# Second norm's scale applied after the feed-forward products in a two-model transformer kernel, with buffers and weight splits moved to suit

## Chip, cores and metric

The kernel runs on one core of a Trainium2 chip. Its metric is the device time of one execution in microseconds (us), the median of three runs. TensorE is PE in the rows, VectorE DVE, ScalarE ACT, GpSimd POOL, SyncE SP.

## What is computed

Two transformer layers, then a second model's block (gated delta rule and dilated attention). Only the layers are touched. Per layer, on x of 512 tokens by 1024:

```python
def rms_norm(x, g):
    xf = x.astype(jnp.float32)
    y = xf * lax.rsqrt(jnp.mean(xf * xf, axis=-1, keepdims=True) + EPS)
    return (y * g.astype(jnp.float32)).astype(x.dtype)

for l in range(DEPTH):                       # DEPTH = 2
    h = rms_norm(x, norm1[l]); proj = h @ w_in[l]
    ...                                      # four attention groups a, b, c, d
    mixed = jnp.concatenate([o_a, o_b, o_c, o_d], axis=-1)
    x = x + mixed @ w_out[l]
    h2 = rms_norm(x, norm2[l])
    x = x + jnp.square(jax.nn.relu(h2 @ w_up[l])) @ w_down[l]
```

## The kernel before

Nearly all work is matmuls of 128 by 128 by 512. For fp32 accuracy each operand is a pair: a high part rounded to fp32r and the rest (low). `product` (L180) issues three matmuls for one product: high by high (L182), high by low (L183), low by high (L184).

**Weights** stream in items of 512 KB through `WeightRing` (L99). SP sends an item into one of four raw slots once the item four earlier is split (L141). ACT rounds it into one of three pair slots (`high`, L152), for which the item three earlier must be used up by PE. DVE subtracts for the low part (`low`, L161). `high(act, i)` and `low(dve, i)` bring the split up to item i + 2. All engines work their queues in order, and the order is written out by hand: a wait holds everything behind it on its engine.

**Front**: the projections of the first norm; PE, ACT and DVE weave 26 weight steps with other work by a table. Its last step is finished inside attention, at p = `HOLD` = 1 (`held`).

**Attention** (L665): 64 jobs in 32 pairs. In round p, PE issues the scores of pair p (L701, L704), the values product of pair p - 4 (L737) and the transposes of pair p - 3 (L718). Scores of pair p need the exps of pair p - 2 done, since there are four score banks. DVE takes the maximum (L768), negates and scales it (L774), inverts the sum (L801); ACT exponentiates (L856) and copies (L865); POOL normalises (L895). Every eight jobs one chunk of `mixed` is stored, high by ACT (L870), low by DVE (L806), into `operand`. `fill` lets PE compute one chunk of the output product (12 matmuls) at p = 34 and at p = 35, after the transposes; it needs all exps done (the banks 0 to 3) and that chunk stored.

**Output product and second norm** (`OutputProducts`, `Residual`): columns 0 to 511 are products over chunks 0 to 7 into banks 0 to 3. Then columns 512 to 1023 into banks 4 to 7: one weight item for all four token tiles, then the last three items tile by tile (18 matmuls each). After each tile DVE adds to x (L603), ACT squares and sums (L452), DVE adds the halves (L457), ACT takes the root (L462), DVE inverts (L468) and scales the whole row (L477), PE transposes it (L505, 8 at a time, behind the next tile's matmuls), ACT and DVE store high (L514) and low (L526) in `operand`. The last tile's transposes have no matmuls left to hide behind; PE issues 24 and 36 dummy matmuls around them (`keep_busy`, L96) and then waits for all of `operand`.

**Feed-forward** (`mlp`): two halves of the 4096 hidden features, each an up projection (`UpProjection`, relu and square) and a down product added to x (L1315; the last half in `finish_dve`, L603), followed by the next norm with the same code. In layer 1 that tail norms twice (L472, L492).

Of the kernel before, what the change touches and what calls it, by code (L numbers as in the profile page):

```python
# [25 lines left out]
F32 = mybir.dt.float32  # L26
# [378 lines left out]
class Norm:  # L405
# [5 lines left out]
    def __init__(self, psum, x, weights, ident, eps, small, work, operand, sems, again=None, ident_half=None):  # L411
# [7 lines left out]
        self.again = again  # L419
# [115 lines left out]
class Residual(Norm):  # L535
# [49 lines left out]
    def add(self, dve, c, t, end, gate=None):  # L585
# [17 lines left out]
        dve.tensor_tensor(self.x[:, t, cols], prod, self.x[:, t, cols], ALU.add).then_inc(self.summed, 1)  # L603
# [61 lines left out]
def attention(block, psum, jobs, stores, ident, ident_half, probs, probs_t, stats, sems, besides=None, ready={},  # L665
# [24 lines left out]
    def _(pe):  # L690
# [51 lines left out]
        for p in range(pairs + STORE + 1):  # L742
# [16 lines left out]
            if fill is not None and p in (pairs + TURN - 1, pairs + VALUES - 1):  # L759
                fill(pe)  # L760

    @block.vector
    def _(dve):
# [59 lines left out]
        for p in range(pairs + STORE + 1):  # L823
# [21 lines left out]
    def _(act):  # L845
# [26 lines left out]
        for p in range(pairs + STORE + 1):  # L872
# [48 lines left out]
def product_by_channels(pe, psum, banks, weights, pair, chunks, written=None):  # L921
# [3 lines left out]
    for i in range(2):  # L925
        w = weights.take(pe)
        n = w[0].shape[1]
        for h, bank in enumerate(banks):
            for kk in range(n):
                if written is not None and h == 0:  # L930
# [3 lines left out]
                             stop=(k + kk == chunks - 1))  # L934
        k += n
# [19 lines left out]

class OutputProducts:
# [5 lines left out]
    def __init__(self, part, prefix, psum, x, weights, ident, ident_half, eps, small, work, lhs, per_half):  # L962
        self.per_half, self.weights, self.lhs, self.psum = per_half, weights, lhs, psum
        self.block = part.block
        self.tail = Residual(psum, x, weights, ident, eps, small, work, lhs, part.sems(prefix, TAIL_SEMS),
                             ident_half=ident_half)
        self.first = self.start = None

    def first_half(self, pe, stored_low, banks_freed):

        k, self.start = 0, self.weights.taken
        for i in range(self.per_half):
            w = self.weights.take(pe)
            for kk in range(w[0].shape[1]):
# [3 lines left out]
                for t in range(T):  # L978
                    tile = slice(t * P, (t + 1) * P)
                    mm = product(pe, self.psum[:, t, 0:w[0].shape[2]], [self.lhs[:, k, j, tile] for j in (0, 1)],  # L980
                                 [w[j][:, kk, :] for j in (0, 1)], start=(k == 0), stop=(k == KD - 1))
# [3 lines left out]
                yield  # L985

# [7 lines left out]

    def rest(self, rows_read, gain_row):
        start, per_half, weights, tail = self.start, self.per_half, self.weights, self.tail

        @self.block.sync
        def _(sp):
            weights.send(sp, start + 1)  # L1000
            sp.wait_ge(*rows_read)
            tail.load_gain(sp, gain_row)
            weights.send(sp, start + 2 * per_half - 1)
            tail.gain_loaded(sp)
# [2299 lines left out]
```

## Time and profile before

| | |
|---|---|
| median of 3 runs | 2093.86 us (2090.22 to 2101.56) |
| profiled execution | 2088.93 us |
| its span | 2087.2 us |
| mean granted TensorE clock | 0.987 |
| PE busy | 2009.6 us, 96% |
| DVE, ACT, POOL busy | 53%, 40%, 17% |
| DMA queue of the weights | 196.53 MB, 30.7% of 16 engines' span |

The span is the profiled execution without what lies around it (1.7 us). PE's busy time counts each matmul from its start to a modelled end, and these overlap; so 96% says that PE seldom stands still, not how much of its time is needed.

### The profile page before, as it was taken

To read this page: it belongs to the slowest core of one execution; us is meant where nothing else is said; L and a number is where in the kernel's file an instruction comes from. 1 tells how busy PE (TensorE), PEld (TensorE's weight loads), DVE (VectorE), ACT (ScalarE), POOL (GpSimd) and SP (SyncE) were. 2 spreads that over 40 slices of the span, in tenths; PEclk is the share of its full clock that TensorE was granted. 3 is DMA by queue.
4 is the path that set the end of the run, shared out by engine and by line. 5 is a ranking of instruction groups with operands and counts; after the bars stand their busy time and mean duration, and the time that the engine had idled before them with its cause. 6 is when DMAs were issued, how large, how long until landed. Compare 5 with 4: busy or idle time off the path is not lost. (4 is left out here: it accounts for less than half of the span.)

```text
span 2087.2 us, 27674 instructions
## 1 busy us (share of the span) xinstructions
PE 2009.6 (96%) x10604; PEld 1618.6 (78%) x10608; DVE 1115.6 (53%) x2039; ACT 836.0 (40%) x1744; POOL 360.1 (17%) x345
## 2 busy tenths in 40 slices
PE   8999999999999999999999999899999999999997
PEld 7776588888887877567888888688787887886776
DVE  5788634423434489835542543579765331425555
ACT  4455634312323344653321332454433334534632
POOL 1336700000000153750000000003030320004300
PEclk9999999999999999999999999999999999999999
DMA  6321022323232432012543433232225323341232
GB/s 190 98 75 52 1 71 92 110 93 91 91 120 71 121 100 80 11 41 81 192 162 93 170 118 111 75 101 83 79 77 146 79 66 99 92 140 41 81 121 81
DMA packets 177524, 198.29 MB, mean 95 GB/s; under 512 B 38755, under 2 KB 140786, under 8 KB 176882
## 3 DMA queue, kind: packets, MB, share of 16 engines
q1 hardware_dynamic: 177394, 196.53, 30.7%
q8 instruction: 85, 1.39, 0.3%
q14 instruction: 45, 0.37, 0.1%
HBM read 180.74 MB, written 11.55 MB: 92 GB/s over the span
## 5 line engine op out<-in xcount | busy, mean ns | idle before, releaser
L161 DVE TENSOR_TENSOR weight_pairs<-weight_ring,weight_pairs 128x1024 fp32r<-128x1024 f32 (+4 forms) x293 | 355.7, 1216 | 411.6 <-ACT weight_pairs L152 411.1
L182 PE MATMUL psum<-operand,weight_pairs 128*128 128x512 f32 x1320 | 526.8, 399 | 12.4 <-PEq L230 8.8
L152 ACT ACTIVATE weight_pairs<-weight_ring 128x1024 fp32r<-128x1024 f32 (+4 forms) x293 | 303.4, 1038 | 538.5 <-PE psum L184 523.6
L184 PE MATMUL psum<-operand,weight_pairs 128*128 128x512 f32 x1320 | 517.2, 392 | 0.0
L183 PE MATMUL psum<-operand,weight_pairs 128*128 128x512 f32 x1320 | 517.1, 392 | 0.0
L182 PEld LDWEIGHTS psum<-operand,weight_pairs 128*128 128x128 f32 x1320 | 249.3, 189 | 72.8 <-issue 19.4
L184 PEld LDWEIGHTS psum<-operand,weight_pairs 128*128 128x128 f32 x1320 | 248.6, 188 | 53.6
L183 PEld LDWEIGHTS psum<-operand,weight_pairs 128*128 128x128 f32 x1320 | 249.2, 189 | 50.9 <-issue 1.0
L895 POOL TENSOR_SCALAR probs<-probs,stats 128x128 f32<-128x128 f32 (+3 forms) x176 | 160.9, 930 | 239.4 <-DVE stats L801 239.1
L182 PE MATMUL psum<-weight_pairs,hidden 128*128 128x512 f32 x512 | 200.8, 392 | 0.0
L184 PE MATMUL psum<-weight_pairs,hidden 128*128 128x512 f32 x512 | 199.9, 391 | 0.0
L183 PE MATMUL psum<-weight_pairs,hidden 128*128 128x512 f32 x512 | 199.7, 390 | 0.0
L182 PE MATMUL psum<-weight_pairs,operand 128*128 128x512 f32 (+3 forms) x384 | 141.2, 368 | 6.1 <-DVE weight_pairs L161 4.6
L1191 DVE TENSOR_TENSOR mlp_work<-mlp_work 128x512 f32<-128x512 f32 x64 | 44.0, 687 | 183.9 <-ACT mlp_work L1174 183.9
L184 PE MATMUL psum<-weight_pairs,operand 128*128 128x512 f32 (+3 forms) x384 | 137.0, 357 | 0.0
L183 PE MATMUL psum<-weight_pairs,operand 128*128 128x512 f32 (+3 forms) x384 | 137.0, 357 | 0.0
L182 PEld LDWEIGHTS psum<-weight_pairs,hidden 128*128 128x128 f32 x512 | 96.5, 188 | 20.3 <-issue 0.2
L183 PEld LDWEIGHTS psum<-weight_pairs,hidden 128*128 128x128 f32 x512 | 96.6, 189 | 20.2 <-issue 0.2
L184 PEld LDWEIGHTS psum<-weight_pairs,hidden 128*128 128x128 f32 x512 | 96.4, 188 | 20.2
L856 ACT ACTIVATE probs<-psum,stats 128x128 f32<-128x128 f32 (+3 forms) x176 | 82.4, 479 | 30.0 <-DVE stats L774 26.0
L1174 ACT ACTIVATE mlp_work<-psum 128x512 f32<-128x512 f32 x64 | 37.6, 594 | 138.2 <-PE psum L184 138.2
L768 DVE TENSOR_REDUCE stats<-psum 128x1 f32<-128x128 f32 (+3 forms) x176 | 66.3, 418 | 39.5 <-PE psum L704 31.1
(417 smaller groups left out, 2709.9 us busy)
## 6 DMA issues: line engine op xcount, KB each, us to landing
weight_ring<-in_w_in_dram SPq DMA_DIRECT2D x100, 512.0 KB, 3.7
weight_ring<-in_w_up_dram SPq DMA_DIRECT2D x64, 512.0 KB, 3.6
weight_ring<-in_w_down_dram SPq DMA_DIRECT2D x64, 512.0 KB, 3.6
weight_ring<-in_w_out_dram SPq DMA_DIRECT2D x24, 512.0 KB, 3.6
ada_rows<-in_ada_w_dram SPq DMA_DIRECT2D x24, 512.0 KB, 4.6
spilled<-v_t SPq DMA_DIRECT2D x22, 256.0 KB, 4.4
weight_ring<-in_w_in_dram SPq DMA_DIRECT2D x20, 256.0 KB, 2.9
weight_ring<-in_w_proj_a_dram SPq DMA_DIRECT2D x8, 512.0 KB, 3.5
```

The source lines that it names most:

```text
L152: act.activation(self.pairs[:, i % SPLIT_RING, 0, 0:n], self.buf[:, i % RING, 0:n], ACT.Copy).then_inc(self.rounded, 1)
L161: dve.tensor_tensor(self.pairs[:, i % SPLIT_RING, 1, 0:n], self.buf[:, i % RING, 0:n], self.pairs[:, i % SPLIT_RING, 0, 0:n].bitcast(F32), ...
L182: pe.matmul(out, lhs[0], rhs[0], start=start, stop=False)
L183: pe.matmul(out, lhs[0], rhs[1], start=False, stop=False)
L184: return pe.matmul(out, lhs[1], rhs[0], start=False, stop=stop)
L768: dve.tensor_reduce(stats[:, 4, j:j + 1], psum[:, j % SB, 0:jobs[j].width], AX_X, ALU.max).then_inc(found, 1)
L856: act.activation(probs[:, j % PB, 0:job.width], psum[:, j % SB, 0:job.width], ACT.Exp, bias=stats[:, 0, j:j + 1], scale=job.scale, accum_o ...
L895: pool.tensor_scalar(rows, rows, stats[:, 2, j:j + 1], None, ALU.mult).then_inc(normed, 1)
L1174: act.activation(self.relu[:, g % B, :], self.psum[:, g % 8, :], ACT.Relu).then_inc(self.rectified, 1)
L1191: dve.tensor_tensor(self.square[:, f % B, :], self.relu[:, f % B, :], self.relu[:, f % B, :], ALU.mult).then_inc(self.squared, 1)
```

## The change

- `OutputProducts` gets code of its own in place of `Residual`. x is multiplied by the norm's gain only, transposed and stored; the division is left out. As relu then square turns a row's factor r into r squared, DVE computes 1 / (mean + eps) per row after the last store (`factor`) and the adds after the down products multiply by it (`scalar_tensor_tensor`). There is no root in this stage.
- The row is scaled, transposed and stored by halves of 512 columns, 4 transposes at a time. The columns 0 to 511 go through while PE computes columns 512 to 1023; the last four transposes go behind the first 12 matmuls of the up projection, which begins when half of `operand` is stored. `keep_busy` is gone here.
- `operand` is written while the second half is multiplied, so chunks 0 to 3 of `mixed` have a buffer of their own. It takes the place of the first eight tiles of `turned_qk`, which are split off (`Tiles`).
- `best` grows from 8 to 32 columns and `small` from 32 to 96. Against before, the buffers behind `small` start 256 bytes later; `latents`, `position_table`, `latent_t`, `probs`, `gate_work` and `stats` start at another remainder of 256 bytes (by 96), and the first eight tiles by 128.
- `fill` runs at p = 32, 33 and 34.
- The split in the last front step (the second item of the output weights) moves from p = 1 to p = 5 of attention on ACT and DVE (`HOLD + T`).
- Before the last tile, ACT and DVE split the next items (first of `w_up`) ahead of that tile's square and add.

```diff
+        if self.factor is None:
+            dve.tensor_tensor(self.x[:, t, cols], prod, self.x[:, t, cols], ALU.add).then_inc(self.summed, 1)
+        else:
+            dve.scalar_tensor_tensor(out=self.x[:, t, cols], in0=prod, scalar=self.factor[:, t:t + 1],
+                                     in1=self.x[:, t, cols], op0=ALU.mult, op1=ALU.add).then_inc(self.summed, 1)
...
-            if fill is not None and p in (pairs + TURN - 1, pairs + VALUES - 1):
+            if fill is not None and p in range(pairs, pairs + TURN):
...
+            if p == HOLD + T and held is not None:
+                held["low"](dve)
...
+            if p == HOLD + T and held is not None:
+                held["high"](act)
...
     for i in range(2):
         w = weights.take(pe)
         n = w[0].shape[1]
+        if ready:
+            pe.wait_ge(*ready[i])
...
+            if between is not None and (i, h) == (0, 0):
+                between(pe)
...
+    def turn(self, pe, c, t):
+        n = T * c + t
+        pe.wait_ge(self.scaled, n + 1)
+        if c:
+            pe.wait_ge(self.low_rows, T if t < 2 else T + t - 1)
+        for k in range(4):
+            mm = pe.transpose(self.bank(c, t)[:, k, :], self.scaled_rows[:, n % self.SLOTS, k * P:(k + 1) * P], self.ident[:])
+        mm.then_inc(self.turned, 1)
...
+    def second_half(self, pe):
+        weights, k = self.weights, 0
+        for i in range(self.per_half - SPLIT_RING):
...
+        for t in range(T - 1):
+            self.turn(pe, 0, t)
...
+        for t in range(T):
+            for i in range(SPLIT_RING):
...
+            if t < T - 1:
+                mm.then_inc(self.tile_done, 1)
+            if t:
+                self.turn(pe, 1, t - 1)
+            else:
+                self.turn(pe, 0, T - 1)
...
+        dve.tensor_tensor(self.x[:, t, cols], self.psum[:, T * c + t, :], self.x[:, t, cols], ALU.add).then_inc(self.summed, 1)
...
+        dve.tensor_tensor(self.scaled_rows[:, n % self.SLOTS, :], self.x[:, t, cols], self.gain[:, cols],
+                          ALU.mult).then_inc(self.scaled, 1)
...
         @self.block.scalar
         def _(act):
-            tail.finish_act(act, start, per_half)
+            for i in range(per_half + 1):
+                weights.high(act, start + i)
+            for t in range(T):
+                self.square(act, 0, t)
+            weights.high(act, start + per_half + 1)
+            for t in range(T):
+                self.high(act, 0, t)
+            for t in range(T):
+                if t == T - 1:
+                    weights.high(act, end - SPLIT_RING + 1)
+                    weights.high(act, end - SPLIT_RING + 2)
+                self.square(act, 1, t)
+                if t:
+                    self.high(act, 1, t - 1)
+            self.high(act, 1, T - 1)
...
+            for t in range(T):
+                if t == T - 1:
+                    weights.low(dve, end - SPLIT_RING + 1)
+                self.add(dve, 1, t)
+                if t == T - 1:
+                    weights.low(dve, end - SPLIT_RING + 2)
+                if t:
+                    self.low(dve, 1, t - 1)
+            self.low(dve, 1, T - 1)
+            own = Chain(dve, self.mean_own)
+            dve.wait_ge(self.squared, 2 * T)
+            own(dve.tensor_tensor(self.mean, self.halves[0], self.halves[1], ALU.add))
+            own(dve.tensor_scalar(self.mean, self.mean, 1.0 / D, EPS, ALU.mult, ALU.add))
+            own(dve.reciprocal(self.factor, self.mean))
...
-        pe.wait_ge(*input_ready)
-        up_1.products(pe)
+        up_1.products(pe, ((output.low_rows, T), input_ready), output.last_turn)
```

PE at the end of the output product of layer 0, and into the up projection. Before:

```order
L184 MATMUL psum<-weight_pairs,operand 128x512
L505 MATMUL psum<-ident,turned_qk 128x128 x8
L96 MATMUL psum<-ident_half 128x128 x24
L505 MATMUL psum<-ident,turned_qk 128x128 x8
L96 MATMUL psum<-ident_half 128x128 x36
L1288 UNCONDITIONAL_BRANCH
L182 MATMUL psum<-operand,weight_pairs 128x512
```

With the change (the dots are 11 more matmuls):

```order
L184 MATMUL psum<-weight_pairs,operand 128x512
L1028 MATMUL psum<-ident,turned_qk 128x128 x4
L1448 UNCONDITIONAL_BRANCH
L182 MATMUL psum<-operand,weight_pairs 128x512
...
L1028 MATMUL psum<-ident,turned_qk 128x128 x4
```

The last tile's transposes now stand among the matmuls of the up projection, and no dummies are left.

ACT at the start of layer 0's attention (rounds p = 1 to 6). Before:

```order
L856 ACTIVATE probs,stats<-psum,stats 128x256 x2
L152 ACTIVATE weight_pairs<-weight_ring 128x1024
L1610 ACTIVATE values<-psum 128x384 x2
L856 ACTIVATE probs,stats<-psum,stats 128x384 x2
L865 ACTIVATE probs_t<-psum 128x128 x2
```

With the change:

```order
L862 ACTIVATE probs,stats<-psum,stats 128x256 x2
L1774 ACTIVATE values<-psum 128x384 x2
L862 ACTIVATE probs,stats<-psum,stats 128x384 x2
L871 ACTIVATE probs_t<-psum 128x128 x2
...
L862 ACTIVATE probs,stats<-psum,stats 128x256 x2
L152 ACTIVATE weight_pairs<-weight_ring 128x1024
L871 ACTIVATE probs_t<-psum 128x512 x2
```

The split (L152) has moved behind the exps of pair 5; DVE's half (L161) moved likewise.

ACT in the norm behind the feed-forward part of layer 0. Before:

```order
L452 ACTIVATE mlp_work,small<-x_stream 128x512
L462 ACTIVATE small<-small,eps 128x1
L452 ACTIVATE mlp_work,small<-x_stream 128x512
```

With the change:

```order
L452 ACTIVATE mlp_work,small<-x_stream 128x512
L462 ACT_TABLE_LOAD
L462 ACTIVATE small<-small,eps 128x1
L452 ACTIVATE mlp_work,small<-x_stream 128x512
```

The load of the root's table, which stood in the output stage, now stands here, in both layers.

## Rows read from the trace of the kernel before

**Rows 1.** Page, section 1: busy time, share of span, instructions

```profile
PE 2009.6 (96%) x10604; PEld 1618.6 (78%) x10608; DVE 1115.6 (53%) x2039; ACT 836.0 (40%) x1744; POOL 360.1 (17%) x345
```

**Rows 2.** Busy time by stage (then PEclk, DMA share, GB/s): layer 0's second norm

```profile
286.80:318.60 31.80, 29.43 (x191) 24.66 (x189) 20.02 (x32) 16.63 (x34) 0.00 (x0) 1.00 0.12 37
```

**Rows 3.** Timeline of PE, layer 0: start us, us, instruction [idle before <-releaser]

```profile
267.74 0.50 PE L182 MATMUL psum<-weight_pairs,operand 128*128 128x512 f32 x1
...
288.95 0.39 PE L182 MATMUL psum<-weight_pairs,operand 128*128 128x512 f32 x1
...
294.85 0.39 PE L184 MATMUL psum<-weight_pairs,operand 128*128 128x512 f32 x1
...
301.31 1.09 PE L505 MATMUL psum<-ident,turned_qk 128*128 128x128 f32 x8 [0.58 <-DVE turned_qk L477]
...
306.12 0.39 PE L184 MATMUL psum<-weight_pairs,operand 128*128 128x512 f32 x1
...
307.15 0.48 PE L182 MATMUL psum<-weight_pairs,operand 128*128 128x512 f32 x1
...
315.07 1.09 PE L505 MATMUL psum<-ident,turned_qk 128*128 128x128 f32 x8 [1.36 <-DVE turned_qk L477]
...
318.60 0.50 PE L182 MATMUL psum<-operand,weight_pairs 128*128 128x512 f32 x1 [0.43 <-DVE operand L526]
```

**Rows 4.** Timelines of DVE and ACT in the same stage

```profile
311.53 0.69 DVE L603 TENSOR_TENSOR x_stream<-psum,x_stream 128x512 f32<-128x512 f32 x1 [0.29 <-PE psum L184]
314.93 1.28 DVE L526 TENSOR_TENSOR operand<-psum,operand 128x512 fp32r<-128x512 f32 x2
...
298.14 1.28 ACT L462 ACT_TABLE_LOAD   x1
315.76 1.09 ACT L514 ACTIVATE operand<-psum 128x512 fp32r<-128x512 f32 x2 [0.35 <-PE psum L505]
```

**Rows 5.** Timelines and one stretch, start of attention, layer 0, then PE in layer 1

```profile
177.22 1.33 DVE L161 TENSOR_TENSOR weight_pairs<-weight_ring,weight_pairs 128x1024 fp32r<-128x1024 f32 x1 [1.24 <-ACT weight_pairs L152]
181.07 0.57 ACT L856 ACTIVATE probs<-psum,stats 128x384 f32<-128x384 f32 x1
181.88 1.19 PE L701 MATMUL psum<-turned_qk 96*128 96x128 f32 x4 [3.20 <-ACT probs L856]
188.57 1.46 PE L701 MATMUL psum<-turned_qk 96*128 96x384 f32 x4
181.88:188.57 6.69, 6.69 (x34) 5.03 (x35) 4.51 (x20) 3.22 (x13) 6.47 (x6) 0.56 0.01 2
183.46 5.54 POOL L895 TENSOR_SCALAR probs<-probs,stats 128x384 f32<-128x384 f32 x4 [0.22 <-DVE stats L801]
839.27 0.77 PE L701 MATMUL psum<-turned_qk 96*128 96x128 f32 x4 [3.09 <-ACT probs L856]
844.80 1.46 PE L701 MATMUL psum<-turned_qk 96*128 96x384 f32 x4
```

**Rows 6.** Timelines of PE, ACT and DVE at the end of attention, layer 0

```profile
260.00 0.66 PE L737 MATMUL psum<-probs_t,values 128*64 128x128 f32 x8 [0.77 <-ACT probs_t L865]
262.10 0.88 PE L737 MATMUL psum<-probs_t,values 128*64 128x128 f32 x12 [0.63 <-ACT probs_t L865]
263.77 0.48 PE L182 MATMUL psum<-weight_pairs,operand 128*128 128x512 f32 x1
258.61 0.70 ACT L856 ACTIVATE probs<-psum,stats 128x512 f32<-128x512 f32 x1
269.46 1.23 DVE L161 TENSOR_TENSOR weight_pairs<-weight_ring,weight_pairs 128x1024 fp32r<-128x1024 f32 x1 [0.26 <-ACT weight_pairs L152]
```

**Rows 7.** PE in the norms behind the feed-forward parts; a DVE group by shape

```profile
658.78 1.04 PE L505 MATMUL psum<-ident,mlp_work 128*128 128x128 f32 x8
1343.69 1.97 PE L505 MATMUL psum<-ident,mlp_work 128*128 128x128 f32 x8 [4.42 <-DVE mlp_work L492]
L2973 DVE SCALAR_TENSOR_TENSOR qk<-psum,cols,qk 128x512 f32<-128x512 f32 x8 | 5.4, 744 | 3.5 <-PE psum L2877 3.5
```

More of the change, by code:

```diff
@@ L978, in first_half @@
                 for t in range(T):
-                    tile = slice(t * P, (t + 1) * P)
-                    mm = product(pe, self.psum[:, t, 0:w[0].shape[2]], [self.lhs[:, k, j, tile] for j in (0, 1)],
-                                 [w[j][:, kk, :] for j in (0, 1)], start=(k == 0), stop=(k == KD - 1))
+                    mm = self.one(pe, t, k, w, kk)
                 k += 1
@@ L985, in first_half, with one @@
                 yield
+    def one(self, pe, bank, k, w, kk):
+        tile = slice((bank % T) * P, (bank % T + 1) * P)
+        return product(pe, self.psum[:, bank, :], [self.lhs[k][:, j, tile] for j in (0, 1)],
+                       [w[j][:, kk, :] for j in (0, 1)], start=(k == 0), stop=(k == KD - 1))
     def fill(self, stored_low, banks_freed):
@@ new lines, in high, with low @@
+    def high(self, act, c, t):
+        act.wait_ge(self.turned, T * c + t + 1)
+        act.activation(self.operand[:, 4 * c:4 * c + 4, 0, t * P:(t + 1) * P], self.bank(c, t), ACT.Copy).then_inc(self.high_rows, 1)
+    def low(self, dve, c, t):
+        dve.wait_ge(self.high_rows, T * c + t + 1)
+        out, high = (self.operand[:, 4 * c:4 * c + 4, j, t * P:(t + 1) * P] for j in (1, 0))
+        dve.tensor_tensor(out, self.bank(c, t), high.bitcast(F32), ALU.subtract).then_inc(self.low_rows, 1)
@@ L1001, in _ @@
             sp.wait_ge(*rows_read)
-            tail.load_gain(sp, gain_row)
-            weights.send(sp, start + 2 * per_half - 1)
-            tail.gain_loaded(sp)
+            sp.dma_start(self.gain, gain_row.to_broadcast([P, D])).then_inc(self.gain_landed, 16)
+            weights.send(sp, end - 1)
+            sp.wait_ge(self.gain_landed, 16)
         @self.block.tensor
@@ L1069, in layers @@
                         begin if l == 0 else None)
-                mixed = operand
+                first_group.close()
+                mixed = sb("mixed", [P, KD // 2, 2, S], mix, F32R)
+                lhs = [mixed[:, c, :, :] for c in range(KD // 2)] + [operand[:, c, :, :] for c in range(KD // 2, KD)]
                 with ExitStack() as ctx:
@@ L1091, in layers @@
                 work = sb("mlp_work", [P, 3, D], ctx)
-                mlp(layer, f"mlp_{l}", (output.tail.low_rows, 2 * T), psum, x, weights, operand, hidden, KH, work, n_down // 2,
+                mlp(layer, f"mlp_{l}", output, psum, x, weights, operand, hidden, KH, work, n_down // 2,
                     ident, ident_half, eps, small,
@@ L1095, in layers, with __init__, __getitem__ @@
         lay.close()
+class Tiles:
+    def __init__(self, first, others):
+        self.first, self.others = first, others
+    def __getitem__(self, key):
+        rows, tile, *cols = key
+        start = tile.start if isinstance(tile, slice) else tile
+        if start < BQ:
+            return self.first[(rows, tile, *cols)]
+        moved = slice(tile.start - BQ, tile.stop - BQ) if isinstance(tile, slice) else tile - BQ
+        return self.others[(rows, moved, *cols)]
 class Modulation:
@@ L1197, in squares, with mlp @@
         self.rest(dve, self.n - 1)
-def mlp(part, prefix, input_ready, psum, x, weights, operand, hidden, n, work, per_half, ident, ident_half, eps, small, gain_row,
+def mlp(part, prefix, output, psum, x, weights, operand, hidden, n, work, per_half, ident, ident_half, eps, small, gain_row,
         besides=(None, None)):
@@ L1223, in mlp @@
     tail = Residual(psum, x, weights, ident, eps, small, work, operand, sems[:n_tail], again, ident_half)
+    tail.factor = output.factor
     @block.sync
@@ L1314, in _ @@
                 cols = slice(c * 512, (c + 1) * 512)
-                dve.tensor_tensor(x[:, t, cols], psum[:, 4 * c + t, :], x[:, t, cols], ALU.add).then_inc(summed_1, 1)
+                dve.scalar_tensor_tensor(out=x[:, t, cols], in0=psum[:, 4 * c + t, :], scalar=output.factor[:, t:t + 1],
+                                         in1=x[:, t, cols], op0=ALU.mult, op1=ALU.add).then_inc(summed_1, 1)
         up.squares(dve, modulation)
@@ L1429, in front @@
     swapped = (swapped_0, swapped_1, swapped_2, swapped_3)
+    n_dense = order.count("dense")
+    held["high"] = lambda act: weights.high(act, base + n_dense - 1)
+    held["low"] = lambda dve: weights.low(dve, base + n_dense - 1)
     def steps():
```

109 lines of the change are left out of this document (83 added, 26 removed).

## The prediction

> **What bounds the kernel now.** I read the page first, then the timelines of each engine at the three places that the change touches. PE is busy for 2009.6 of 2087.2 us [rows 1], so only two things shorten the kernel: PE standing still less, or PE doing less that isn't needed. The busy share hides the second. In layer 0's second norm PE counts as busy for 29.43 of 31.80 us [rows 2], yet 60 dummy matmuls are in there, and transposes during which no product runs. So I count matmuls. The pitch of products is (294.85 - 288.95) / 26 = 0.227 us [rows 3]. From the second chunk of the output product at 267.74 to the first matmul of the up projection at 318.60 there are 7 x 12 + 96 = 180 products, 40.8 us; the time is 50.86 us, so 10.0 us are not products. The rows show where: PE waits 0.58 us for the first scaled tile (ACT loads the root's table just then, 1.28 us [rows 4]), 1.36 for the last one, 0.43 for the last store, and dummies fill the rest. In this stage a chain over DVE and ACT ends last, from the last tile's product to its stored operand.
>
> At the start of attention PE waits 3.20 us for the exps of pair 2. They come late since DVE first waits 1.24 us for ACT's split, then splits (1.33), then copies, and only then takes the maxima [rows 5]. [...] At the end of attention PE waits 0.77 and 0.63 us for ACT's copies while the output product's chunks are held back [rows 6].
>
> **The change part by part.**
>
> *Second norm.* Of the 10.0 us I take 0.2 as slower pitches that stay. Eight transposes cost (307.15 - 306.12) - 0.23 = 0.80, with the slower matmul behind them 0.89 [rows 3]: some 0.10 each and 0.09 for a change of kind. The change makes the same 32: 12 together (1.3) and five times 4 (0.49 each, 2.5), so 3.7 us by estimate. Is anything else waited for? Call T the end of the last tile's products. Its four transposes of columns 0 to 511 are long done. DVE adds and multiplies (2 x 0.69 [rows 4]), ready by T + 1.7. PE does four transposes and 12 matmuls of the up projection, to T + 3.3, so it doesn't wait. The transposes end at T + 3.8, ACT stores the high half-row (half of 1.09), DVE the low one (half of 1.28), T + 5.1; PE needs them after 12 more matmuls at T + 6.5: 1.4 us to spare. What DVE holds ahead of it, a split of 1.23 and another low half, fits before the transposes end. Per tile DVE has 0.69 + 0.69 + 0.64 = 2.0 us of work against PE's 18 x 0.227 + 0.49 = 4.6. The split of the first up item comes before the last add, as its item is freed a third into the last tile. The gain row's transfer is issued behind the same sends as before and has some 10 us before it is read. So 10.0 - 0.2 - 3.7 = **6.1 us per layer, 12.2 in both**; bounds 4 (each of the four late turns waits half a microsecond) and 6.6 (a change of kind costs nothing).
>
> *Split moved from p = 1 to p = 5.* [...] The 6.69 us up to the scores at 188.57 are 6.69 x 0.56 = 3.7 of work at full clock; but POOL then needs 5.54 us for the four normalisations of pairs 2 and 3, and each pair of scores waits for exps, so I add 1.5. The scores start at 184.7, 3.9 us earlier (bounds 2.5, only the wait, and 5.4, no new wait). In layer 1 the wait was 0.1 shorter and the stretch 5.53 us [rows 5], so 2.6. At p = 5 the split costs up to 1.06 + 1.23 us of DVE before the maxima of pair 6; DVE and ACT have gaps there, and I take 0.7 per layer (bounds 0 and 2.3). Sum 3.9 + 2.6 - 1.4 = **5.1 us**, bounds 0 and 8.
>
> *Fill at p = 32 to 34.* The first chunk needs all exps: the last starts at 258.61 and takes 0.70, so 259.4 in place of 263.77 [rows 6]. The waits of 0.77 and 0.63 are then covered, less 0.2 of new waiting: 1.2. But chunk 4 needs an item whose split stands behind attention's last store. Its low part ended at 269.46 + 1.23, 2.9 us after the last values product; after the change PE reaches it some 2.7 us after that product. I take off 0.4: **0.8 per layer, 1.6**; bounds 0 and 2.8.
>
> *Root's table.* The loads at the second norm go, and the orders show them again in the norm behind the feed-forward part. In layer 0 PE reaches the first turn there without a wait [rows 7]. With 1.28 us more it waits as in the output stage, 0.7. In layer 1 the two norms make a chain with DVE at its end (PE waits 4.42 us for the last tile), so all 1.3 counts. **Minus 2.0**, bounds 0.6 and 4 (a longer wait in layer 1 may hold the clock low longer; the last transposes there already take 1.97 instead of 1.09). [...]
>
> *Adds with a factor.* The nearest operation, one PSUM and one SBUF source with a per-row scalar, takes 0.744 [rows 7], the plain add 0.69. Most are hidden; in layer 1's tail four are on the chain and in layer 0's one or two. **Minus 0.3**, bounds 0 and 1. The three small operations for the factor stand where DVE waits for ACT anyway, and PE needs DVE's next split 5 us later: nothing.
>
> *Buffers.* Separate chunks of `mixed` cost no instruction. At a new remainder of 256 bytes stand the operands of attention's matmuls and POOL's `probs`. No two rows of the trace show one operation at two remainders and a different time, so I take nothing, with a bound of 3% of the 82 us from 181.88 to 263.77 [rows 5, 6] either way, 5 us in both layers.
>
> **Sum.** 12.2 + 5.1 + 1.6 - 2.0 - 0.3 = 16.6 us. Against the profiled execution 2088.93 becomes 2072.3. That execution lies 4.9 us below the median of the three runs; from the median 2093.86 it is **2077 us**, 0.8% less. About 0.5%, 10.5 us, is what a measurement of this kernel can tell from no change.
>
> **Rivals.**
>
> *The wait moves to p = 5, and layer 1's tail grows.* DVE's split reads two SBUF operands while POOL normalises. If they shut each other out, POOL loses 1.23 us or DVE 5.54 / 4 = 1.4 us, then pairs 6 and 7 are late and the clock falls as it did at pair 4: the 5.1 us are gone. With the tail at its bound of 4 the gain is 12.2 + 1.6 - 4.3 = 9.5, so 2084. For it: POOL is busy 6.47 of 6.69 us there. Against: the split at 177.22 took 1.33, only 0.1 over its 1.23. [...]
>
> [...]
>
> *The new remainders cost what the start of attention gains.* If they slow attention's operations by 3%, the 4.9 us of that bound go, and 16.6 - 4.9 = 11.7 are left, 2082. For it: every `probs` row, and the tiles of the first 16 jobs, stand elsewhere. Against: no row shows such a dependence.
>
> [...]
>
> **How the numbers follow.** As summed 0.66, the moved wait 0.15, waits at the turns 0.06, remainders 0.05, more 0.08. The range takes in the case as summed with its bounds and part of the spread of the runs (2090 to 2102 before), the case of more, the remainders and the moved wait: 2067 to 2087. Outside are the slower case and the ends of the others, under 2 in 10. Faster by over 0.5% (below 2083.4): 0.66 x 0.94 + 0.08 + 0.15 x 0.35 + 0.05 x 0.6 = 0.78. Slower by over 0.5%: 0.04, out of the waits at the turns. The rest, 0.18, is no change.
>
> **What would show it.** From the last product of the output stage to the first of the up projection there should be about 0.7 us, with no wait at L1028 over 0.3, and 25 to 26 us where rows 2 have 31.80 (6.1 less, and the last four transposes lie behind its end). PE should wait about 0.7 us at pair 4 of attention, and the clock stay at 1.00 there. The first output chunk should start 4.4 us earlier against the values products. The table load should stand in the last norms, with PE waiting 0.5 to 1 us at the first turn in layer 0. The prediction is wrong if the transposes at L1028 wait for `scaled` or for the low stores, if rounds 6 to 9 of attention wait over 1 us for exps, or if operations on `probs` take another time than before.

## The result, and the profile after

The changed kernel takes 2067.34 us, median of 4 runs (2065.72 to 2071.46), against 2094.51 for the kernel before on the same chip: ratio 0.9868, interval 0.9845 to 0.9892. The forecast was 2077 with 2067 to 2087, out of a base of 2093.86; that base times 0.9868 is 2066.2, just below the range. The direction and the places were right, the gain is some 10 us larger than the 16.6 summed. Run twice more (e1, g3), the same code gave 2070.93 and 2072.19. The 15 executions have a median of 2070.3, the 81 of the kernel before 2093.9: a gain of 23.6 us, 1.1%. Later kernels are compared with 2070.3 where nothing else is said; the kernel before has medians from 2092.5 to 2096.4 on the five chips of the experiments, so 2 us between two chips mean little. The spans of the two profiled executions are 2087.2 and 2064.0 us, 23.2 apart.

Page of the changed kernel, section 1, for [rows 1]:

```profile
PE 1996.0 (97%) x10484; PEld 1606.1 (78%) x10488; DVE 1118.0 (54%) x2037; ACT 834.6 (40%) x1736; POOL 361.2 (17%) x345
```

PE has 120 instructions less, the 60 dummies per layer. Timeline of PE in layer 0's norm, for [rows 3]:

```profile
287.45 1.47 PE L1028 MATMUL psum<-ident,turned_qk 128*128 128x128 f32 x12
...
292.89 0.60 PE L1028 MATMUL psum<-ident,turned_qk 128*128 128x128 f32 x4
...
302.01 0.60 PE L1028 MATMUL psum<-ident,turned_qk 128*128 128x128 f32 x4
302.37 0.48 PE L182 MATMUL psum<-weight_pairs,mixed 128*128 128x512 f32 x1
302.68 0.40 PE L183 MATMUL psum<-weight_pairs,mixed 128*128 128x512 f32 x1
...
306.57 0.60 PE L1028 MATMUL psum<-ident,turned_qk 128*128 128x128 f32 x4
306.93 0.48 PE L182 MATMUL psum<-operand,weight_pairs 128*128 128x512 f32 x1
...
309.77 0.60 PE L1028 MATMUL psum<-ident,turned_qk 128*128 128x128 f32 x4
310.13 0.48 PE L182 MATMUL psum<-operand,weight_pairs 128*128 128x512 f32 x1
```

No row ends in a bracket: PE waits for none of its turns (a turn is one such set of transposes). Four transposes cost 0.36 us, and the matmul behind them takes 0.08 more than the pitch; that is 0.44 where I took 0.49. From the last product's end at 306.57 to the first up product 0.36 us pass. Before, two sets of transposes (the last at 315.07, [rows 3]) and two runs of dummies lay between them, 7.3 us (311.33 to 318.60). What runs meanwhile on DVE and ACT, for [rows 4]:

```profile
307.57 0.69 DVE L1092 TENSOR_TENSOR turned_qk<-x_stream,turned_qk 128x512 f32<-128x512 f32 x1
...
311.04 0.69 DVE L1070 TENSOR_TENSOR operand<-psum,operand 128x512 fp32r<-128x512 f32 x1 [1.04 <-ACT operand L1065]
311.65 0.15 DVE L1152 TENSOR_TENSOR small<-small 128x4 f32<-128x4 f32 x1
...
310.41 0.60 ACT L1065 ACTIVATE operand<-psum 128x512 fp32r<-128x512 f32 x1 [1.70 <-PE psum L1028]
```

The last low part ends 5.2 us behind the last product's end (I had 5.1), and PE needs it 12 matmuls after 310.13, at 313.0: 1.2 us to spare. Attention's start, PE and one stretch of it (us, then busy us of PE, PEld, DVE, ACT, POOL, PEclk, DMA share, GB/s), for [rows 5]:

```profile
179.48 0.68 PE L705 MATMUL psum<-turned_qk_first 96*128 96x128 f32 x4 [0.62 <-ACT probs L862]
...
181.80 1.10 PE L705 MATMUL psum<-turned_qk_first 96*128 96x256 f32 x4 [0.46 <-ACT probs L862]
...
179.48:184.24 4.76, 4.30 (x34) 3.21 (x35) 4.04 (x18) 3.00 (x13) 4.55 (x5) 1.00 0.00 0
825.86 0.68 PE L705 MATMUL psum<-turned_qk_first 96*128 96x128 f32 x4 [0.62 <-ACT probs L862]
...
186.87 1.23 DVE L161 TENSOR_TENSOR weight_pairs<-weight_ring,weight_pairs 128x1024 fp32r<-128x1024 f32 x1 [1.47 <-ACT weight_pairs L152]
```

The wait of 3.20 us is 0.62 now, the clock stays at 1.00, and the split at p = 5 takes 1.23 us beside POOL. At its end, for [rows 6], the first chunk starts at 255.30 (I had 4.4 us earlier against the values products; with the 4.2 us that layer 0 had gained by then it is 4.3):

```profile
255.30 0.47 PE L182 MATMUL psum<-weight_pairs,mixed 128*128 128x512 f32 x1 [0.27 <-issue]
```

The feed-forward tails, for [rows 7]: the table load on ACT, then PE's turns in layer 0 and in layer 1.

```profile
645.23 1.28 ACT L462 ACT_TABLE_LOAD   x1
648.39 1.09 PE L505 MATMUL psum<-ident,mlp_work 128*128 128x128 f32 x8 [0.65 <-DVE mlp_work L477]
...
1303.07 1.09 PE L505 MATMUL psum<-ident,mlp_work 128*128 128x128 f32 x8 [3.67 <-DVE mlp_work L492]
...
1323.88 1.20 PE L505 MATMUL psum<-ident,mlp_work 128*128 128x128 f32 x8 [4.49 <-DVE mlp_work L492]
```

**Where the 23.2 us come from.** I matched PE's instructions of the two traces in order and followed the difference of their start times (changed minus before). Such matched starts are the landmarks below. The difference is -4.20 us at the end of layer 0's attention, -11.20 at the first product over `hidden` (405.77 before, 394.57 after), still -11.20 at the end of the feed-forward part, -10.40 behind its tail, -11.00 at the start of layer 1's attention (0.6 came back in layer 1's front, where PE's wait before one product is 1.05 us in place of 1.66), -14.05 at the end of layer 1's attention, -21.08 behind its norm, -20.41 at 1385, and -23.25 at 1983 of the kernel before. So attention gives 4.20 and 3.05, norm and fill together 7.0 in each layer, the tails take 0.20 and 0.67, and 2.84 arise in the second model's block, which the change doesn't touch.

### The profile page after: what moved, and what is told of

Same layout as the page of the kernel before. It is cut to its first block and busy times, and to the rows that moved or that the text cites. A ratio compares the mean times of both kernels' runs of the same rounds, so it can differ in the third digit from the quotient of the medians.

```text
span 2064.0 us, 27440 instructions
## 1 busy us (share of the span) xinstructions
PE 1996.0 (97%) x10484; PEld 1606.1 (78%) x10488; DVE 1118.0 (54%) x2037; ACT 834.6 (40%) x1736; POOL 361.2 (17%) x345
## 5 line engine op out<-in xcount | busy, mean ns | idle before, releaser
L161 DVE TENSOR_TENSOR weight_pairs<-weight_ring,weight_pairs 128x1024 fp32r<-128x1024 f32 (+4 forms) x293 | 355.7, 1216 | 397.0 <-ACT weight_pairs L152 395.9
L152 ACT ACTIVATE weight_pairs<-weight_ring 128x1024 fp32r<-128x1024 f32 (+4 forms) x293 | 303.5, 1038 | 525.2 <-PE psum L184 510.6
L182 PE MATMUL psum<-weight_pairs,operand 128*128 128x512 f32 (+3 forms) x320 | 115.7, 362 | 5.7 <-DVE weight_pairs L161 4.1
L183 PE MATMUL psum<-weight_pairs,operand 128*128 128x512 f32 (+3 forms) x320 | 112.1, 350 | 0.0
L184 PE MATMUL psum<-weight_pairs,operand 128*128 128x512 f32 (+3 forms) x320 | 112.1, 350 | 0.0
```

The costliest lines, as they stand in the source:

```text
L152: act.activation(self.pairs[:, i % SPLIT_RING, 0, 0:n], self.buf[:, i % RING, 0:n], ACT.Copy).then_inc(self.rounded, 1)
L161: dve.tensor_tensor(self.pairs[:, i % SPLIT_RING, 1, 0:n], self.buf[:, i % RING, 0:n], self.pairs[:, i % SPLIT_RING, 0, 0:n].bitcast(F32), ...
L182: pe.matmul(out, lhs[0], rhs[0], start=start, stop=False)
L183: pe.matmul(out, lhs[0], rhs[1], start=False, stop=False)
L184: return pe.matmul(out, lhs[1], rhs[0], start=False, stop=stop)
```

## Experiments

Theory: each part gives what its landmarks say, and the surplus over my sum is attention's start (7.3 for 5.1) and chance in the granted clock. Rivals: the parts help each other; the buffers' places, priced at nothing, give some of it.

### The parts alone

**f9** keeps the norm and undoes the other two parts:

```diff
-                if d < n_dense - 1:
-                    weights.high(act, base + d)
+                weights.high(act, base + d)
...
-            if p == HOLD + T and held is not None:
-                held["high"](act)
...
-            if fill is not None and p in range(pairs, pairs + TURN):
+            if fill is not None and p in (pairs + TURN - 1, pairs + VALUES - 1):
```

(and the same for `low` on DVE).

> The changed kernel with both other parts undone: the split at p = 1 and the chunks at p = 34 and 35. What is left against the kernel before is the norm (my 12.2 us), the root's table in the tails (0.7 by the trace, 2.0 by my sum), the adds with a factor and the buffers: 10 to 11.5 us less than before, ratio 0.9948 to 0.9953. If the parts help each other (the clock stays up only with all of them), it is 8 us or less. By the landmarks the output stage and its norm should take 6.1 us less in each layer.

Measured: 2083.96 us, 12 runs, ratio 0.9959 (0.9944 to 0.9974), 9 us less than before. The first products over `hidden` of this kernel, then those of the kernel before, in both layers:

```profile
399.56 0.39 PE L182 MATMUL psum<-weight_pairs,hidden 128*128 128x512 f32 x1
...
1060.78 0.39 PE L182 MATMUL psum<-weight_pairs,hidden 128*128 128x512 f32 x1
```

```profile
405.77 0.39 PE L182 MATMUL psum<-weight_pairs,hidden 128*128 128x512 f32 x1
...
1062.04 0.39 PE L182 MATMUL psum<-weight_pairs,hidden 128*128 128x512 f32 x1
```

Against the kernel before, the difference at the end of attention was +0.10 us in layer 0 and +5.08 in layer 1, so the norm is worth 6.31 and 6.34 us. Layer 1's attention began at -5.0; the 10 us lost in it are low clock, 23.9 us of it at half speed against 3.4 in the kernel before (more below). The norm's term stands, 12.65 for my 12.2.

**e2** is the complement, the kernel before with split and fill:

```diff
+            if p == HOLD + T and held is not None:
+                held["low"](dve)
...
-            if fill is not None and p in (pairs + TURN - 1, pairs + VALUES - 1):
+            if fill is not None and p in range(pairs, pairs + TURN):
```

(and the same for `high` on ACT; the front leaves that item out).

> The kernel before with two of the change's parts, the split moved to p = 5 and the chunks filled at p = 32 to 34, and the old norm. By the offsets between the two traces the split is worth 4.0 (layer 0) and 2.9 us (layer 1), by my sum the fill 0.8 per layer: 8.5 us less than the kernel before, ratio 0.996, so that the norm's part would be the larger rest. If the parts depend on each other (the fill pays only when the norm behind it is short) it is 6 to 7 us. If the norm's part was under-priced and the split over-priced, under 6.

Measured: 2081.89 us, ratio 0.9944 (0.9925 to 0.9964), 10.6 us less than before on its chip. By landmarks the split gives 4.3 us in layer 0 and 3.1 in layer 1, the fill 0.6 in each. 9 and 10.6 add to 19.6 of the 23.6: no large help between the parts. **e4** undoes the fill alone (the last edit of f9's diff):

> The changed kernel with the chunks at p = 34 and 35 only. By my sum PE then waits 0.77 and 0.63 us for ACT's copies again and covers none of it: 0.8 us per layer, 1.6 in all, ratio to the kernel before 0.9876. Rival: without the chunk at p = 33 the first item of the output product is freed later, and the splits behind it come later: up to 2.8 us per layer. Rival: nothing, as the output product has the same matmuls in either order and PE catches up.

Measured: 2071.28 us, which can't be told from the changed kernel; the landmarks show +0.68 us in layer 0 and +0.69 in layer 1. So the fill is worth 1.4 for my 1.6, and only the trace can tell. **e3** undoes the split alone (f9's first edits):

> The changed kernel with the last front item split at p = 1 again. Theory (the wait at pair 4 costs itself and the clock behind it): PE waits some 3.2 us again at pair 4, the granted clock falls to about 0.56 behind it, layer 0's attention ends 4.0 us later and layer 1's 2.9 us, so 7 us slower than the changed kernel, ratio to the kernel before 0.990. Rival (the moved split mostly trades one wait for another): 2 to 3 us slower, 0.988.

Measured: 2082.64 us, 9 runs, ratio 0.9938 (0.9916 to 0.9960): 12 us slower than the changed kernel, more than either theory. PE of e3 in layer 1's start, then of the kernel before at the same place, where the code is the same:

```profile
838.13 0.68 PE L705 MATMUL psum<-turned_qk_first 96*128 96x128 f32 x4 [3.09 <-ACT probs L860]
...
840.45 2.04 PE L705 MATMUL psum<-turned_qk_first 96*128 96x256 f32 x4 [0.46 <-ACT probs L860]
...
845.02 2.29 PE L705 MATMUL psum<-turned_qk_first 96*128 96x384 f32 x4
```

```profile
839.27 0.77 PE L701 MATMUL psum<-turned_qk 96*128 96x128 f32 x4 [3.09 <-ACT probs L856]
...
841.72 1.74 PE L701 MATMUL psum<-turned_qk 96*128 96x256 f32 x4
844.80 1.46 PE L701 MATMUL psum<-turned_qk 96*128 96x384 f32 x4
```

After the same wait of 3.09 us the low clock lasted longer here: the last group takes 2.29 us in place of 1.46. Against e1 the start costs e3 4.6 us in layer 0 and 5.4 in layer 1. So moving the wait away is worth 3 to 5.4 us a layer, by how long the clock stays low behind it, and my one trace showed the short case in layer 1. The two add to 10 us; e3's median is 12 above.

### What comes by chance

**e1** and **g3** are the changed kernel itself.

> The changed kernel once more, unaltered. After layer 1 it had gained another 2.3 us on the kernel before, in the second model's block, whose code is the same in both. Theory P (placement): the stretches of lowered granted clock (0.84 to 0.88 over some 12 us each) fall where the program puts them; then this execution shows them within a slice of the same times, and the second block takes the same time within 0.5 us. Rival C (chance): they fall elsewhere in each execution, and the second block's time moves by 1 to 3 us. The median should lie at 2066 to 2069 by either.

> The changed kernel unaltered, a third time on a chip. Its median was 2067.34 in the first runs and 2070.93 in e1, where two of six executions lay 6 us above the others, the size of one fall of the clock in the middle of attention. If such falls come by chance, at the same place and in some executions, this set has again a group at 2065 to 2071 and single ones 6 us above; the median is 2066 to 2071. If e1's chip was slower as a whole, all executions shift alike.

Measured: 2070.93 us (2069.57 to 2077.16) and 2072.19 (2067.70 to 2076.87). Chance it is. Up to 867 us e1's trace runs within 0.4 us of the first one; then this stretch of e1, and the same work in the first execution:

```profile
864.00:866.00 2.00, 2.00 (x16) 0.83 (x14) 0.40 (x1) 0.89 (x4) 1.82 (x2) 1.00 0.00 0
866.00:868.00 2.00, 2.00 (x20) 1.11 (x16) 2.00 (x9) 1.46 (x5) 0.10 (x1) 0.95 0.00 0
868.00:880.00 12.00, 12.00 (x56) 6.82 (x55) 5.03 (x19) 4.28 (x15) 7.21 (x7) 0.50 0.01 1
```

```profile
222.00:236.00 14.00, 13.74 (x114) 7.78 (x112) 7.10 (x28) 9.33 (x34) 11.23 (x11) 1.00 0.01 2
```

(the second is layer 0 of the changed kernel, the same jobs). PE stood busy throughout and waited for nothing, yet the clock fell to 0.50 for some 13 us and the attention took 6.1 us longer. Such a fall is in 7 of the 38 attentions of all 19 profiles (I had miscounted them as 6 of 30 when I wrote h2's expectation), always at the jobs of group d, whose scores have a second matmul over 2 rows (`gates`), and it begins within half a microsecond of one place of the program in each layer. The untouched second block is as variable: against the kernel before it gained 2.8 us in the first trace, 3.0 in f9's, 0.4 in e2's. In the changed kernel's own repeats it gained -0.1 (e1) and 2.9 (g3), of the same code. Its stretch 1950 to 2000 has a clock of 0.93 in e1 and 0.97 in g3.

**h1** and **h2** try the version that looked fastest (e5, below) and, on top, dummies where the falls begin:

```diff
+            if held is not None and 18 <= p <= 21:
+                keep_busy(pe, psum[:, 2 * p % SB, :], ident_half, 6)
```

> e5's kernel a second time, as the candidate. Outside the falls of the clock it should keep its gain on the changed kernel, by landmarks 0.9 to 1.1 us over layer 0's feed-forward tail and 0.4 us over layer 1's; its median is that of the changed kernel (2070.3 over 15 executions) less 1.3 us, 2069, give or take 2 us for the falls that chance puts into the set.

> The same with 6 dummy matmuls ahead of the scores in rounds 18 to 21 of each attention, 24 in all at 0.054 us, 1.3 us per layer. There the falls to half clock began, some 14 us long and 5.8 us each, in 6 of the 30 attentions looked at. Theory L (PE's narrow matmuls of group d leave the clock at the edge, and chance decides): with the dummies no execution has such a fall, the executions lie within 3 us of each other, and the median is 2069 to 2071, no better than without them. Rival: the falls have nothing to do with what PE does in these rounds; they stay as frequent, and the median is 2071 to 2074.

Measured: h1 2067.53 us (2066.28 to 2083.22), h2 2070.96 (2070.37 to 2077.03). In h2 five of six executions lie within 2 us, in h1 two of six lie 7 and 16 us above the rest. That fits theory L, but h2 has one at 2077.03, and six executions don't settle it. Its one trace has no fall, and neither has that of h1, without the dummies. What decides the falls stays open. The dummies buy no time on the median.

### The root's table

**e5** loads the table early, behind the squares of the first half in each tail (`spare` is an unused column):

```diff
         for t in range(T):
             self.square_half(act, 0, t)
+        act.activation(self.spare, self.eps[:, 0:1], ACT.Sqrt)
```

> The changed kernel with one root of a constant on ACT in each feed-forward tail, behind the squares of the first half, so that the root's table is loaded there and not at the first root of the norm. My sum put the load on the path with 0.7 us in layer 0 and 1.3 in layer 1: by it 2.0 us are gained back. The trace of the changed kernel showed offsets of only 0.2 and 0.5 us over those tails, so the rival is 0.7 us. In both, PE's wait at the first turn should fall from 0.65 us to about 0 in layer 0 and from 3.67 to 2.4 in layer 1. If a load costs nothing wherever it stands, both waits stay as they are.

Measured: 2065.62 us; with h1's runs 2067.4 over 10 executions, 2.9 below the changed kernel's 2070.3 (f12 below, which has the same edit, has 2070.52). So few runs can't tell it from equal, though the trace can:

```profile
615.59 1.28 ACT L641 ACT_TABLE_LOAD   x1
647.30 1.04 PE L506 MATMUL psum<-ident,mlp_work 128*128 128x128 f32 x8
...
1300.55 1.09 PE L506 MATMUL psum<-ident,mlp_work 128*128 128x128 f32 x8 [2.58 <-DVE mlp_work L493]
...
1321.30 1.97 PE L506 MATMUL psum<-ident,mlp_work 128*128 128x128 f32 x8 [4.48 <-DVE mlp_work L493]
```

The waits behave as summed: 0.65 to none, 3.67 to 2.58. Layer 0 gains 0.85 us. In layer 1 the chain runs 1.1 us earlier to the last turn, but that turn takes 1.97 us at low clock in place of 1.20, and 0.4 is left. In h1's trace, of the same kernel, the tails give 0.85 and 1.4. It is the best version found by the traces, 1.2 to 2.2 us; the times don't show it.

### The buffers' places

**e6** takes the padding of `best` away, **e7** that of `small`:

```diff
-                best = sb("best", [P, 32], mix)[:, 0:8]
+                best = sb("best", [P, 8], mix)[:, 0:8]
```

```diff
-        small = sb("small", [P, 96])
+        small = sb("small", [P, 36])
```

> The changed kernel with `best` 8 columns wide, so that latents and probs_t stand at 32 bytes and probs, gate_work, stats at 96, as before the change (and the first eight tiles and mixed at 32 in place of 128). If remainders are worth the 3% of attention that I took as a bound, attention's 82 us per layer change by 2.5 us; if they don't matter, every group of attention has the same mean duration within 1% and the landmarks agree within 0.3 us outside falls of the clock.

> The changed kernel with `small` 36 columns wide in place of 96: all buffers behind it lie 240 bytes lower, so 16 bytes off the remainder of 256 that they had in both kernels (the weights, x and operand, allocated ahead, stay). If the padding that the change adds is needed, DVE, ACT and POOL operations on probs, hidden, mlp_work take another time and the kernel is slower by 5 us or more; if not, means agree within 1% and the median within 2 us.

Measured: e6 2071.34 us, its landmarks 0.4 us late in each layer behind the products over `mixed`, whose pitch is 0.2335 us there against 0.229; e7 **2087.84 us** (10 runs), 17 us slower. The groups of DVE, ACT and POOL kept their means but for small differences (all their busy time together differs by 1.0 us from e1's). PE's pitch did not. Layer 0's 384 matmuls over `hidden`, first one and the matmul behind the last, in the changed kernel, then in e7 (by the allocated addresses `small` takes 160 bytes there for its 144, so all behind it moved by 224 bytes and not 240, 32 off the old remainder and not 16):

```profile
394.57 0.39 PE L182 MATMUL psum<-weight_pairs,hidden 128*128 128x512 f32 x1
...
481.61 0.39 PE L182 MATMUL psum<-operand,weight_pairs 128*128 128x512 f32 x1
```

```profile
394.60 0.39 PE L182 MATMUL psum<-weight_pairs,hidden 128*128 128x512 f32 x1
...
484.19 0.39 PE L182 MATMUL psum<-operand,weight_pairs 128*128 128x512 f32 x1
```

From start to start that is (481.61 - 394.57) / 384 = 0.2267 us against 0.2333. The busy time of one matmul, 0.39 in both, doesn't show it. Three more kernels ask what decides: **f10** and **g1** (`small` with 80 and 64 columns), and **g2**, which moves the other operand:

```diff
         x = sb("x_stream", [P, T, D])
+        sb("pad_0", [P, 32])
         weights = WeightRing(nc, ctx)
...
-        small = sb("small", [P, 96])
+        small = sb("small", [P, 64])
```

> The changed kernel with `small` 80 columns wide: everything behind it lies 64 bytes lower (hidden, y_pair and mixed at 64 of 256 bytes in place of 128). [...]

> The changed kernel with `small` 64 columns wide: hidden, y_pair and mixed at 0 of 256 bytes. So far the pitch of products that read hidden was 0.2267 us at 128 (changed kernel), 0.2290 at 64 (f10), 0.2333 at 160 (e7), and for y_pair 0.2267, 0.2333, 0.2333. Theory R (the distance to the other operand, weight_pairs at 128, decides, and equal remainders are best): at 0 the pitch is 0.2290 or more and the kernel 6 to 17 us slower. [...]

> The changed kernel with weight_ring, weight_pairs and operand 128 bytes further on (at 0 of 256), and `small` 32 columns narrower, so that all behind it stays (hidden at 128). By theory R the products over hidden now have unequal remainders and slow to 0.2290 or more, while products of operand with weight_pairs, both moved, keep 0.2272: some 5 to 10 us slower. [...]

Measured, with the distance of the buffer from `weight_pairs` by the allocator's addresses, modulo 256 bytes:

| kernel | distance | pitch over `hidden` | over `y_pair` | median us |
|---|---|---|---|---|
| changed | 0 | 0.2267 | 0.2267 | 2070.3 |
| f10 | -64 | 0.2289 | 0.2333 | 2078.45 |
| g1 | -128 | 0.2324 | 0.2333 | 2085.22 |
| g2 | +128, `hidden` not moved | 0.2324 | 0.2333 | 2090.27 |
| e7 | +32 | 0.2333 | 0.2333 | 2087.84 |

The rows of g2 behind its value:

```profile
394.88 0.40 PE L182 MATMUL psum<-weight_pairs,hidden 128*128 128x512 f32 x1
...
484.11 0.39 PE L182 MATMUL psum<-operand,weight_pairs 128*128 128x512 f32 x1
```

Theory R holds: `hidden` stands in the same place in g2 and the changed kernel, and its products take 0.2324 us in place of 0.2267 with the weights moved; products of operand and weights, moved together, keep 0.2272. A place at a multiple of 64 bytes was not enough (f10, at 64 of 256: 0.2289 and 0.2333), and one at 0 of 256 was no better (g1: 0.2324 and 0.2333). So the remainder of one buffer by itself doesn't explain these times, the distance between a matmul's two operands does, and distance 0 was the best seen. The distance alone is not the whole rule: at -64 `y_pair` has the full 0.2333 and `hidden` 0.2289, and the rows name the two operands in the other order.

The pitch also doesn't account for all of the time. Over 1536 products with `hidden` and 336 with `y_pair` it makes 5.6 us in f10, 11 in g1 and g2, and 12.4 in e7. Against kernels on the same chips that keep the distance of 0 (f11, g3, g3 and e6) the medians are 7.1, 13.0, 18.1 and 16.5 us longer. Up to 7 us of that is not traced to a cause. The 192 matmuls over `mixed` have a pitch of 0.229 in the changed kernel, though at distance 0 modulo 256; modulo 512 it is 256, while `hidden` is at 0. That alone is not the reason: in the kernel before `hidden` is at 256 modulo 512 as well, and its pitch is (492.81 - 405.77) / 384 = 0.2267 us. The difference, some 0.5 us, is not traced to a cause.

**f11** puts `ident` (at 32 of 256) to 0, **f12** does so with the early table:

```diff
+    sb("pad_1", [P, 8])
     ident = sb("ident", [P, P])
...
+    sb("pad_2", [P, 8])
     ident_half = sb("ident_half", [P, P], BF16)
...
-        small = sb("small", [P, 96])
+        small = sb("small", [P, 80])
```

> The changed kernel with ident, ones and causal at 0 of 256 bytes in place of 32, and all other buffers where they were. ident is the one fp32 matmul operand that lies off a multiple of 64. If the cost of e7 holds for it too, the transposes, now 0.37 us for 2, 0.59 for 4 and 1.02 for 8, become up to 3% shorter, some 0.02 us a group, 2 to 4 us in all. Rival: what costs is the address of the operand that PE reads as its other input, and ident's makes no difference: same durations, same time.

> e5 and f11 together, as a candidate for the fastest version: the root's table loaded early in both feed-forward tails, ident aligned. By e5's landmarks the table is worth 1.8 us up to 1325 us; with ident's part as in f11. 2063 to 2067 if both count, about 2066 if only the table does.

Measured: 2071.33 and 2070.52 us; the landmarks of f11 agree with the changed kernel's within 0.2 us up to 667, and behind one short fall of the clock at 668 they keep a distance of 1.5 to 1.9. No difference from `ident`'s place shows.

### The order of the splits

**e8** puts the splits of the last two items behind the last tile:

```diff
-                if t == T - 1:
-                    weights.high(act, end - SPLIT_RING + 1)
-                    weights.high(act, end - SPLIT_RING + 2)
                 self.square(act, 1, t)
                 if t:
                     self.high(act, 1, t - 1)
+            weights.high(act, end - SPLIT_RING + 1)
+            weights.high(act, end - SPLIT_RING + 2)
```

(and the same for `low` on DVE).

> The changed kernel with the splits of the last two items behind the last tile's work on ACT and DVE, as the order was before. The first up item then has its low part at about 311.0 us in place of 306.4: after ACT's square, high half and split (0.63 + 0.58 + 1.06 from 307.5) and DVE's 1.23. PE, which starts the up projection at 306.93, waits 4.1 us per layer, 8.2 in both; if the granted clock falls behind the wait as it did behind the 3.20 us at pair 4, another 2 to 3 us each, 14 in all. Rival: the last turn and its stores, which stand in the way anyway, hide half of it, 4 us in all.

Measured: 2083.93 us, 13.6 slower.

```profile
310.93 0.79 PE L182 MATMUL psum<-operand,weight_pairs 128*128 128x512 f32 x1 [3.79 <-DVE weight_pairs L161]
...
310.93:316.00 5.07, 5.07 (x17) 4.13 (x18) 1.08 (x1) 0.01 (x1) 0.00 (x0) 0.66 0.68 205
```

A wait of 3.79 us, then a clock of 0.66: 5.6 us per layer by the landmarks. Of the norm's 6.3 us per layer 0.7 would be left with the old order: without the moved splits the new norm gives little.

## Why the prediction was right or wrong

The mechanisms came as told; what failed is the size of the sum. In the profiled execution 16.6 us came as 23.2. The step that was most wrong is the term of the split: 5.1 us summed from one execution's stretches of low clock, with 0.7 per layer taken off for new waits at p = 5, where the landmarks show 7.3 and, in e3, 10. The tails' price of 2.3 came as 0.9. The last step failed too: the sum was carried over from one profiled execution to the median, although that execution lay below the median and the clock differs from one execution to the next.

| term | predicted | measured by landmarks |
|---|---|---|
| second norm | 12.2 | 12.65 (f9) |
| fill | 1.6 | 1.4 (e4) |
| split moved | 5.1 | 4.2 + 3.1 = 7.3; up to 10 where the clock stays low longer (e3) |
| root's table, adds | -2.3 | -0.9 in the trace; the table alone 0.85 + 0.4 (e5) |
| buffers | 0 | no loss; `best`'s padding is worth 0.4 per layer (e6), an unlucky width of `small` costs 17 (e7) |
| second block | none | +2.8, by chance |
| sum | 16.6 | 23.2 |

- **Norm: right**, in size and in each part. No turn waits, and the spare time was 1.2 us for my 1.4. The slower case, waits at the turns (0.06), did not come; what a wait in this stage costs e8 shows, at another place: 3.79 us, and a clock of 0.66 over the 5.07 us behind it.
- **Fill: right**, 0.7 per layer for 0.8.
- **Split: right in place, mis-sized.** The wait of 0.7 came as 0.62, with a second of 0.46. That PE would go on 2.5 us earlier and at full clock, from which the scores' start at 184.7 is summed, no row of before shows; in the changed kernel PE went on at 179.48, 2.40 us earlier, at a clock of 1.00, and the scores started at 184.24. Wrong was the cost of 0.7 at p = 5: layer 0 kept 4.2 us, more than the 3.9 summed ahead of that cost, so nothing of it shows. Wrong too was to take layer 1's stretch of 5.53 us as the size: e3 and f9 show longer ones. The rival of a wait moved to p = 5 fell: the split there took 1.23 us.
- **Table: right in mechanism, over-priced.** PE's wait in layer 1's tail grew by 1.14 us as summed, but the last turn took 1.20 us in place of 1.97 and gave 0.8 back. In layer 0 the tail took 0.80 for the 0.7 summed, but 0.6 of it came back in layer 1's front, which the sum left out. The adds with a factor took 0.744 to 0.747 us, as read. No further cost shows around the load: it ends at 646.51 and the next activation on ACT starts at 646.53, and taking the load off PE's path shortened the waits by 0.65 and 1.09 us, less than its own 1.28.
- **Buffers: right by luck.** I gave "no row shows it" as an argument for nothing. e7, g1 and g2 are 15 to 20 us slower, with `hidden` and `y_pair` off the distance that this change keeps. My bound named attention's operands; the products that slowed down are those over `hidden` and `y_pair`, in the feed-forward part and the second block.
- **The base.** The profiled execution of the kernel before lay 5 us below its median, that of the changed kernel 1.6 below. I carried the sum over to the median unchanged. These 3.4 us and the second block's 2.8, both of them what single executions happened to have, are 6 of the 10 us of surplus. How much of the 23.6 us between the medians belongs to the removed waits beyond what the first trace shows can't be told apart from chance with these runs.

## What to carry to other kernels

Read a wait's cost as the wait plus the low clock behind it, and from several executions: the same 3.09 us cost 3 us in one and 5.4 in another. Before buffers are moved, write down the distance of each pair of matmul operands modulo 256 bytes (over `hidden` and `y_pair` 0 gave 0.2267 us, the others 0.2289 to 0.2333), and measure the pitch from start to start, since busy times don't show it (0.39 us at 0.2267 and at 0.2333). When products are to start at once behind a stage, put the split of their first item ahead of that stage's last tile: here 5.6 of the new norm's 6.3 us per layer hung on this order.

## What was not expected of the hardware

- The pitch of a 128x512 matmul depends on how its two operands lie to each other: 0.2267 us over `hidden` and `y_pair` at distance 0 modulo 256 bytes, 0.2289 to 0.2333 (up to 2.9% more) in the four kernels with other distances.
- The granted clock can fall to 0.50 for 13 us while PE is busy without a gap, at the same place of the program, in 7 of 38 passages and not in the others.
- Single executions of one kernel differ by up to 21 us (2085.81 to 2106.56 before, over all chips), and the span goes with the mean granted clock: on one chip 2087.0 us at 0.987, 2103.3 at 0.978.
